# Forget sums and causal mask of a prompt's attention: from matrix products to copies by DMA and additions by VectorE

## The chip, the cores and the metric

One NeuronCore of a Trainium2 chip runs the whole kernel. The metric is the device time of one launch in microseconds (us).

## What is computed

One decoder layer for a prompt of 512 tokens and for 8 samples of one new token each, in float32. The input projection feeds three branches, the branches are gated and merged, and an output projection with a norm is added to the residual. The change touches only the prompt's attention. Its forgetting branch, with 8 heads of 64:

```
c = jnp.swapaxes(jnp.cumsum(logf, axis=1), 1, 2)                  # (B, 8 heads, 512)
s = einsum('bqhd,bshd->bhqs', qb, k) * scale + cb[..., :, None] - c[..., None, :]
p = _masked_softmax(s, kpos[None, :] <= qpos[:, None])
o = einsum('bhqs,bshd->bqhd', p, v)
```

The term of the query, `cb`, is the same along a row and falls out of the softmax, so the kernel adds only `-c`, one row of 512 values for each head. The sparse branch's selected-block and window attention use the same causal mask without such a term, and the memory branch uses neither.

## The kernel before

The program is a chain of stages, each a block with one instruction stream for each engine. A block ends when all its streams have ended. The ones that matter here are `project` (input projection), `middle`, `prompt` and `sample_and_merge`, in this order.

`middle` (551 us into the run it is over) does small work: the samples' compressed attention and its top-k, the first softmax of the samples' forgetting attention, the hidden layer of the prompt's compressed blocks, and the forget sums. Its SyncE (SP) queue loads weights `w1` into three parts of the tile `oT`: part i%3 holds step i of the four steps of `hidden`, so part 0 (rows 0 to 3 of `oT`) is used by steps 0 and 3, and part 2 (rows 8 to 11) by step 2. TensorE counts the steps in `hidden_done` (L896). VectorE writes the negated cumulative sums of all heads, `k.ncum`, [8 partitions, 512] (L1083). SP also copies a row `imp` (L851) and stores the log forget values (L853, L854) and waits for these stores at its end. The last instruction of the stage is VectorE's copy L1182.

`prompt` works in 56 units. A unit is a pair of heads (j = 0, 1) and a tile of 128 queries; with tile t the unit covers n = 128(t+1) keys, and a set is the four units t = 0 to 3 of one pair. Units 0 to 15 are the forgetting branch ("fox"), 16 to 47 the sparse branch (sets "slc" and "win" by turns), and 48 to 55 the memory branch, which has n = 256 and no mask. For each unit, by engine:

- TensorE, `scores(u)`: query times key (L1311); for fox the product of a one-hot column of the identity, spread over 128 columns, with `k.ncum`, accumulated into the same bank (L1315); then identity times `k.causal`, a 128 by 128 tile of zeros and large negative numbers, accumulated into the last 128 keys (L1319). Each of these is issued twice, once for each head; the trace shows two instructions for one such float32 product, so four in all.
- VectorE, `maximum(u)`: negated maximum over both heads' banks (L1398).
- ScalarE, `exponential(u)`: exponential with the row sum (L1445).
- VectorE, `normalise(u)`: reciprocal (L1402), gate for slc and win (L1405), scaling in place (L1409, twice).
- TensorE, `turn(u)`: transposes (L1330) into banks 4 and 5. VectorE copies those of head 0 to SBUF (`place`, L1416), ScalarE those of head 1 (L1453).
- TensorE, `values`: once a set, probabilities times values (L1350).

The order is written by hand. TensorE runs, for each u: scores(u+2), values of the set that has just ended, four page products (L1363), turn(u). VectorE runs maximum(u+2), normalise(u+1), place(u). ScalarE runs exponential(u+2), place(u). Scores(u+2) wait for the exponentials of u, since two pairs of score banks are used by turns; turn(u) waits for both copies of unit u-1.

The page products belong to the samples of the forgetting branch and ride along in units 4 to 48: 160 pages of 256 KB are loaded by SP (L1296) into eight places, freed pair by pair.

Of the kernel before, what the change touches and what calls it, by code (L numbers as in the profile page):

```python
# [25 lines left out]
ALU = mybir.AluOpType  # L26
# [10 lines left out]
H = 8  # L37
# [719 lines left out]
def middle(k):  # L757
# [4 lines left out]
    with ExitStack() as cx:  # L762
# [50 lines left out]
        grow_done = sem("a_grow_done")  # L813
# [22 lines left out]
        with nc.Block() as block:  # L836
            @block.sync
            def _(sp):
                def load_hidden(i):
                    for v in range(2):  # L840
                        for rows in halves:
                            sp.dma_start(w1[i % 3][rows, v, :, :], k.w_cmp1[0, v][:, i * STEP:(i + 1) * STEP, :]).then_inc(w1_in[i % 3], 16)

                sp.dma_start(bf[:, :], k.b_fgate.rearrange("a h -> h a")).then_inc(b_in, 16)
                sp.dma_start(gsel, k.selectors).then_inc(gsel_in, 16)
                for i in range(3):
                    load_hidden(i)
                sp.wait_ge(hidden_done, 1)
                load_hidden(3)
                sp.wait_ge(imp_out, 2)  # L850
                sp.dma_start(imp[:, :], flat.rearrange("o (n b) -> o n b", n=NG)).then_inc(imp_in, 16)  # L851
                sp.wait_ge(row_out, 2)
                sp.dma_start(rows_of(k.o_logf_p), lrow[:, :, :]).then_inc(out_done, 16)  # L853
                sp.dma_start(k.o_logf_s, k.slrow[:, :]).then_inc(out_done, 16)  # L854
                sp.wait_ge(out_done, 32)
# [344 lines left out]
def prompt(k):  # L1200
# [10 lines left out]
    U = len(units)  # L1211
    ends_group = lambda u: u.last and u.kind != "slc"
# [27 lines left out]
    with ExitStack() as cx:  # L1240
# [17 lines left out]
        pt_left, pt_right, o_done, out_done = (sem("f_" + n) for n in ("pt_left", "pt_right", "o_done", "out_done"))  # L1258
        o_out = [sem(f"f_o_out{i}") for i in range(2)]
        score = lambda u: [ps[2 * (u.no % 2)], ps[2 * (u.no % 2) + 1]]  # L1260
        both = lambda u: k.score_banks[:, 2 * (u.no % 2):2 * (u.no % 2) + 2, 0:u.n]
        pt_bank, o_bank, fv_bank = ps[4:6], ps[6], ps[7]
# [23 lines left out]
        with nc.Block() as block:  # L1286
# [18 lines left out]
            def _(te):  # L1305
                def scores(u):
                    if u.no >= 2:
                        te.wait_ge(e_done, 2 * (u.no - 1))
                    more = u.kind != "mem"
                    for j in range(2):  # L1310
                        last = nc.tensor.matmul(score(u)[j][:, 0:u.n], query(u, j), key(u, j), start=True, stop=not more,  # L1311
                                                skip_group_check=True)
                    if u.kind == "fox":
                        for j in range(2):
                            nc.tensor.matmul(score(u)[j][:, 0:u.n], k.ident[0:H, 2 * u.c + j:2 * u.c + j + 1].to_broadcast([H, P]),  # L1315
                                             k.ncum[:, 0:u.n], start=False, stop=False, skip_group_check=True)
                    if more:
                        for j in range(2):
                            last = nc.tensor.matmul(score(u)[j][:, u.t * P:u.n], k.ident, k.causal, start=False, stop=True,  # L1319
                                                    skip_group_check=True)  # L1320
                    last.then_inc(s_done, 1)
# [73 lines left out]
            def _(ve):  # L1395
                def maximum(u):
                    ve.wait_ge(s_done, u.no + 1)
                    nc.vector.tensor_reduce(nm[:, u.no, :], both(u), AX, ALU.max, negate=True).then_inc(m_done, 1)  # L1398
# [893 lines left out]
def hybrid_step(nc, x_prompt, x_sample, cache_nsa_cmp, cache_nsa_slc, state_nsa_win, cache_fox_kv, cache_fox_logf,  # L2292
# [59 lines left out]
    with ExitStack() as cx:  # L2352
# [20 lines left out]
        k.oT = sb("oT", [P, 12, T])  # L2373
        held, k.slrow = sb("srow", [NB, M_ALL]), sb("slrow", [NB, H])
# [60 lines left out]
```

## Time and profile before

| | |
|---|---|
| median of 3 runs | 1423.58 us (1414.3 to 1429.61) |
| the profiled execution | 1424.95 us |
| its span, first to last instruction | 1423.2 us |
| TensorE busy | 1204.9 us, 85% |
| VectorE busy | 802.0 us, 56% |
| ScalarE busy | 228.5 us, 16% |
| mean granted TensorE clock | 0.915 of full speed |

Busy times of the engines overlap. The profiled execution is one launch with the hardware profiler on; the last row says which share of its full 2.4 GHz TensorE was granted over the span.

### The profile page before, as it was taken

The page shows a single profiled execution, that of the slowest core. Times are in us where ns is not written, and L with a number is a line of the kernel's source. Part 1 is how long each engine was busy: PE and PEld are TensorE (multiplying, and loading weights), DVE is VectorE, ACT ScalarE, POOL GpSimd, SP SyncE. Part 2 cuts the span into 40 slices and gives each one's busy share as a digit, 9 for nine tenths or more (in the row PEclk, how much of TensorE's full clock was granted, in tenths as well). Part 3 has the DMA queues.
Part 4 walks back from the last instruction along what each step waited for, and adds up shares of the span by engine and source line. Part 5 has one row for each costly group of instructions (what it writes and reads, how often), then busy time and mean ns, then how long its engine had stood idle before and what let it go on. Part 6 is the DMA issues. An engine that isn't in the chain of part 4 may idle for free. (4 is left out here: it accounts for less than half of the span.)

```text
span 1423.2 us, 27444 instructions
## 1 busy us (share of the span) xinstructions
PE 1204.9 (85%) x10100; PEld 813.7 (57%) x10100; DVE 802.0 (56%) x1167; ACT 228.5 (16%) x692; POOL 173.1 (12%) x149
## 2 busy tenths in 40 slices
PE   0656677999999577999999888989899799999996
PEld 0655566887888455544444466766556364665542
DVE  1444331298989973335544547676776948544123
ACT  0010041112121111233333410110000000000023
POOL 0000000120000000000000073144051422410000
PEclk9978879999999775699999999999999989998998
DMA  8898524267888632187767194466578767657620
GB/s 221 248 314 240 169 85 148 89 222 217 277 280 295 213 78 75 49 306 226 258 233 233 60 291 152 149 193 229 160 231 260 248 209 234 221 176 270 244 93 31
DMA packets 205900, 282.01 MB, mean 198 GB/s; under 512 B 21749, under 2 KB 126734, under 8 KB 205254
## 3 DMA queue, kind: packets, MB, share of 16 engines
q1 hardware_dynamic: 109958, 202.40, 43.0%
q10 hardware_dynamic: 89376, 60.01, 14.8%
q0 software_dynamic: 6432, 17.83, 3.8%
q8 instruction: 80, 1.31, 0.4%
q14 instruction: 54, 0.44, 0.1%
HBM read 273.26 MB, written 11.11 MB: 200 GB/s over the span
## 5 line engine op out<-in xcount | busy, mean ns | idle before, releaser
L1735 PE MATMUL bank<-xnT,e_wg 128*128 128x260 f32 x1152 | 282.9, 405 | 0.0
L1735 PEld LDWEIGHTS bank<-xnT,e_wg 128*128 128x128 f32 x1152 | 230.8, 203 | 54.5 <-issue 15.8
L585 PE MATMUL score_banks<-xnT,oT 128*128 128x260 f32 (+1 forms) x864 | 196.8, 386 | 8.4 <-DMA oT<-in_w_in 8.4
L1719 POOL DMA_INDIRECT d_slc<-in_cache_nsa_slc,selrow x128 | 154.8, 1210 | 273.5 <-PE score_banks L1811 234.1
L585 PEld LDWEIGHTS score_banks<-xnT,oT 128*128 128x128 f32 (+1 forms) x864 | 161.3, 189 | 38.4 <-DMA oT<-in_w_in 8.7
L249 PE MATMUL score_banks<-c_cols,c_w 64*64 64x64 f32 (+1 forms) x4096 | 97.2, 256 | 96.6 <-issue 58.3
L249 PEld LDWEIGHTS score_banks<-c_cols,c_w 64*64 64x64 f32 x4096 | 92.4, 168 | 101.2 <-issue 101.2
L299 DVE COPY c_cols<-oT 128x1024 f32<-128x1024 f32 x48 | 49.6, 1159 | 92.5 <-DMA oT<-in_cache_nsa_cmp 67.1
L1398 DVE TENSOR_REDUCE f_pt<-score_banks 128x2 f32<-128x512 f32 (+3 forms) x56 | 45.1, 805 | 80.0 <-PE score_banks L1319 78.0
L1743 PE MATMUL bank<-oT,e_wb 128*128 128x512 f32 x192 | 89.0, 607 | 0.0
L1363 PE MATMUL bank<-mt,rpast 128*8 128x512 f32 x320 | 59.9, 601 | 6.1 <-DMA mt<-in_cache_fox_kv 5.0
L1416 DVE COPY f_pt<-bank 128x128 f32<-128x128 f32 (+2 forms) x68 | 27.6, 421 | 61.6 <-PE bank L1330 61.3
L1958 ACT ACTIVATE cst<-bank 128x260 f32<-128x260 f32 x36 | 14.0, 388 | 287.9 <-PE bank L1735 287.8
L1743 PEld LDWEIGHTS bank<-oT,e_wb 128*128 128x128 f32 x192 | 36.2, 194 | 41.9 <-issue 41.3
L2060 DVE TENSOR_REDUCE d_ss<-d_kpage 128x16 f32<-128x1024 f32 (+1 forms) x32 | 56.1, 1754 | 1.1
L2069 DVE TENSOR_TENSOR d_kpage<-d_kpage,d_qrow 128x2048 f32<-128x2048 f32 x24 | 54.7, 2281 | 2.8 <-DMA d_kpage<-in_cache_fox_kv 2.8
L2071 DVE TENSOR_REDUCE rpast<-d_kpage 128x32 f32<-128x2048 f32 x24 | 54.9, 2286 | 0.8
L1445 ACT ACTIVATE mnT<-score_banks,f_pt 128x256 f32<-128x256 f32 (+3 forms) x76 | 38.8, 515 | 79.5 <-DVE f_pt L1398 79.2
L745 DVE TENSOR_TENSOR oT<-oT,p_qrow 128x1024 f32<-128x1024 f32 x40 | 49.0, 1225 | 2.2 <-DMA oT<-in_cache_fox_kv 2.2
L745 DVE TENSOR_TENSOR mt<-mt,p_qrow 128x1024 f32<-128x1024 f32 x40 | 48.9, 1224 | 1.4 <-DMA mt<-in_cache_fox_kv 1.3
L747 DVE TENSOR_REDUCE sfe<-oT 128x16 f32<-128x1024 f32 x40 | 48.8, 1220 | 1.4
L747 DVE TENSOR_REDUCE sfe<-mt 128x16 f32<-128x1024 f32 x40 | 48.8, 1220 | 1.4
(390 smaller groups left out, 1447.1 us busy)
## 6 DMA issues: line engine op xcount, KB each, us to landing
mt<-in_cache_fox_kv SPq DMA_DIRECT2D x240, 256.0 KB, 3.8
d_kpage<-in_cache_fox_kv SPq DMA_DIRECT2D x96, 256.0 KB, 4.4
d_vpage<-in_cache_fox_kv SPq DMA_DIRECT2D x96, 256.0 KB, 3.6
oT<-in_cache_fox_kv SPq DMA_DIRECT2D x80, 256.0 KB, 3.8
e_wg<-in_w_in ACTq DMA_DIRECT2D x36, 512.0 KB, 5.1
oT<-in_cache_nsa_cmp SPq DMA_DIRECT2D x128, 128.0 KB, 3.8
oT<-in_w_in ACTq DMA_DIRECT2D x13, 1024.0 KB, 6.9
oT<-in_cache_nsa_cmp ACTq DMA_DIRECT2D x64, 128.0 KB, 3.7
```

What stands on the lines that cost most here:

```text
L249: return nc.tensor.matmul(hp[s][half][halves[v], 0:n], w1[rows, v, d, :], cols[s][rows, v, d, 0:n], start=d == 0, stop=d == HD - 1)
L299: nc.vector.tensor_copy(dst, src).then_inc(page_free[slot], 1)
L585: last = nc.tensor.matmul(pj[ch.n % 2][i][0:ch.w, 0:NM if ch.mem else TH], w[:, c, ch.off:ch.off + ch.w], rhs, start=c == 0, stop=c == DC - 1)
L745: nc.vector.tensor_tensor(slot, slot, qrow[b % 2][:, :].unsqueeze(1).to_broadcast([P, KR, BRW]), ALU.mult).then_inc(k_times, 1)
L747: nc.vector.tensor_reduce(k.sfe[:, b, g * KR:(g + 1) * KR, :], slot.rearrange("p n (h d) -> p n h d", h=H), AX, ALU.add).then_inc(k_free, 1)
L1363: last = nc.tensor.matmul(fv_bank[32 * i:32 * i + H, :], k.pfe[:, b, page, :], vpage[:, (n % VG) * KV + i % KV, :], start=g == 0, stop=g = ...
L1719: nc.gpsimd.indirect_dma_start(out=slc[:, b % 2, n, :], out_offset=None, in_=k.cache_slc, in_offset=bass.IndirectOffsetOnAxis(ap=k.selrow[ ...
L1735: last = nc.tensor.matmul(gate_bank[n % 2][:, 0:TH], wg[product % WR][:, c, :], k.xnT[:, c, part * TH:(part + 1) * TH], start=c == 0, stop ...
L1743: last = nc.tensor.matmul(z_bank[:, :], wb[n % 2][:, c, :], k.oT[:, (n % 3) * 4 + c, :], start=c == 0, stop=c == 3)
L2060: nc.vector.tensor_reduce(ss[:, first:first + tiles, g * R:(g + 1) * R].rearrange("p n r -> p r n"), product, AX, ALU.add).then_inc(small_ ...
L2069: nc.vector.tensor_tensor(pages, pages, qrow[:, 0, :].unsqueeze(1).to_broadcast([P, KR, BRW]), ALU.mult).then_inc(k_times, 1)
L2071: nc.vector.tensor_reduce(k.pfe[:, b - EARLY, g * KR:(g + 1) * KR, :], pages.rearrange("p n (h d) -> p n h d", h=H), AX, ALU.add).then_inc ...
```

## The change

The forget sums are spread to all partitions beforehand. In `middle`, once `k.ncum` is written (`cum_out`) and the weights in the place concerned are used up, SP issues eight DMAs. Each reads one head's row of `k.ncum`, 2 KB in one partition of SBUF, 128 times and writes it to the 128 partitions of one row of `oT` (heads 0 to 3 to rows 8 to 11 once step 2 of `hidden` is done, heads 4 to 7 to rows 0 to 3 once step 3 is). SP then waits for all eight, and only then issues the stores of the log forget values. In `prompt`, the products L1315 and L1319 are gone. VectorE's `maximum(u)` first adds the spread sums to both score banks in place (fox only, n values for each head), then the causal mask to the last 128 keys of both (all but memory units), each waiting for the one before by a semaphore, and then takes the maximum.

```diff
+                sp.wait_ge(cum_out, 1)
+                for h in range(H):
+                    if h % 4 == 0:
+                        sp.wait_ge(hidden_done, 3 + h // 4)
+                    sp.dma_start(k.bias(h), k.ncum[h:h + 1, :].unsqueeze(1).to_broadcast([1, P, T])).then_inc(bias_in, 16)
+                sp.wait_ge(bias_in, 16 * H)
                 sp.wait_ge(row_out, 2)
                 sp.dma_start(rows_of(k.o_logf_p), lrow[:, :, :]).then_inc(out_done, 16)
...
+    for u in units:
+        u.masks = sum(v.kind != "mem" for v in units[:u.no + 1])
...
+        own_block = lambda u: k.score_banks[:, 2 * (u.no % 2):2 * (u.no % 2) + 2, u.t * P:u.n]
...
-                    more = u.kind != "mem"
                     for j in range(2):
-                        last = nc.tensor.matmul(score(u)[j][:, 0:u.n], query(u, j), key(u, j), start=True, stop=not more,
-                                                skip_group_check=True)
-                    if u.kind == "fox":
-                        for j in range(2):
-                            nc.tensor.matmul(score(u)[j][:, 0:u.n], k.ident[0:H, 2 * u.c + j:2 * u.c + j + 1].to_broadcast([H, P]),
-                                             k.ncum[:, 0:u.n], start=False, stop=False, skip_group_check=True)
-                    if more:
-                        for j in range(2):
-                            last = nc.tensor.matmul(score(u)[j][:, u.t * P:u.n], k.ident, k.causal, start=False, stop=True,
-                                                    skip_group_check=True)
+                        last = nc.tensor.matmul(score(u)[j][:, 0:u.n], query(u, j), key(u, j), start=True, stop=True)
                     last.then_inc(s_done, 1)
...
                     ve.wait_ge(s_done, u.no + 1)
+                    if u.kind == "fox":
+                        forget = k.oT[:, (8 + 2 * u.c) % 12:(8 + 2 * u.c) % 12 + 2, 0:u.n]
+                        nc.vector.tensor_tensor(both(u), both(u), forget, ALU.add).then_inc(biased, 1)
+                    if u.kind != "mem":
+                        if u.kind == "fox":
+                            ve.wait_ge(biased, u.no + 1)
+                        nc.vector.tensor_tensor(own_block(u), own_block(u), k.causal.unsqueeze(1).to_broadcast([P, 2, P]), ALU.add).then_inc(masked, 1)
+                        ve.wait_ge(masked, u.masks)
                     nc.vector.tensor_reduce(nm[:, u.no, :], both(u), AX, ALU.max, negate=True).then_inc(m_done, 1)
...
+        k.bias = lambda h: k.oT[:, (8 + h) % 12, :]
```

## Rows read from the trace of the kernel before

**Rows 1.** Page, part 1: busy time, share of the span, instructions.
```profile
PE 1204.9 (85%) x10100; PEld 813.7 (57%) x10100; DVE 802.0 (56%) x1167; ACT 228.5 (16%) x692; POOL 173.1 (12%) x149
```

**Rows 2.** Prompt's attention: PE, PEld, DVE, ACT, POOL busy; clock, DMA share, GB/s.
```profile
553.00:815.00 262.00, 251.57 (x1319) 119.71 (x1319) 119.95 (x327) 90.53 (x310) 0.00 (x0) 0.91 0.59 195
```

**Rows 3.** Groups of instructions by line, 551 to 815 us: busy, mean ns, idle.
```profile
L1398 DVE TENSOR_REDUCE f_pt<-score_banks 128x2 f32<-128x512 f32 (+3 forms) x56 | 45.1, 805 | 80.0 <-PE score_banks L1319 78.0 <-PE score_banks L1311 1.8
...
L1319 PE MATMUL score_banks<-cst 128*128 128x128 f32 x192 | 38.1, 327 | 0.0
...
L1315 PE MATMUL score_banks<-ncum,cst 8*128 8x128 f32 (+3 forms) x64 | 28.9, 585 | 0.0
```

**Rows 4.** TensorE in order of time, full clock: start, duration (us).
```profile
601.21 0.49 PE L1311 MATMUL score_banks<-fm 64*128 64x128 f32 x4
...
616.85 1.98 PE L1315 MATMUL score_banks<-ncum,cst 8*128 8x512 f32 x4
...
618.75 0.71 PE L1319 MATMUL score_banks<-cst 128*128 128x128 f32 x4
...
619.40 1.04 PE L1363 MATMUL bank<-mt,rpast 128*8 128x512 f32 x8
...
620.96 0.49 PE L1311 MATMUL score_banks<-fm 64*128 64x128 f32 x4
```

**Rows 5.** Groups by shape, 600 to 780 us: busy us, mean ns.
```profile
L1398 DVE TENSOR_REDUCE f_pt<-score_banks 128x2 f32<-128x1024 f32 x10 | 12.3, 1225 | 19.1 <-PE score_banks L1319 19.1
...
L1398 DVE TENSOR_REDUCE f_pt<-score_banks 128x2 f32<-128x256 f32 x10 | 4.2, 424 | 2.6 <-PE score_banks L1319 2.6
```

**Rows 6.** VectorE by shape, whole span: one input in PSUM, and a PSUM write.
```profile
L1106 DVE TENSOR_TENSOR rpast<-rpast,bank 128x1280 f32<-128x1280 f32 x1 | 1.5, 1489 | 0.5 <-PE bank L964 0.5
...
L2178 DVE MEMSET bank<- 128x512 f32 x1 | 0.5, 485 | 1.3 <-PEq L2328 1.3
```

**Rows 7.** TensorE in order of time, 551 to 600 us, half clock.
```profile
551.36 0.80 PE L1311 MATMUL score_banks<-fm 64*128 64x128 f32 x4 [1.71 <-PEq L2328]
...
566.71 3.78 PE L1315 MATMUL score_banks<-ncum,cst 8*128 8x512 f32 x4
570.42 1.22 PE L1319 MATMUL score_banks<-cst 128*128 128x128 f32 x4
...
588.33 4.54 PE L1350 MATMUL bank<-f_pt,row 128*64 128x512 f32 x16
592.79 1.02 PE L1363 MATMUL bank<-mt,rpast 128*8 128x512 f32 x2
```

**Rows 8.** Middle stage in order of time.
```profile
511.13 0.46 SPq L853 DMA_DIRECT2D out<-a_lrow  x1
...
519.94 0.67 DVE L1083 TENSOR_SCALAR ncum<-score_banks 8x512 f32<-8x512 f32 x1
...
521.46 3.38 PE L896 MATMUL bank<-oT,cst 64*8 64x64 f32 x128
...
528.02 0.63 PE L896 MATMUL bank<-oT,cst 64*8 64x64 f32 x32
```

**Rows 9.** End of the middle stage in order of time.
```profile
549.68 0.68 DVE L1182 COPY cst<-bank 64x512 f32<-64x512 f32 x1 [1.16 <-PE bank L995]
```

**Rows 10.** Stretches: DMA share and GB/s, loads into 64 partitions.
```profile
499.00:499.50 0.50, 0.50 (x32) 0.50 (x24) 0.50 (x2) 0.06 (x1) 0.00 (x0) 0.50 1.01 229
```

**Rows 11.** Stretches: the same, pages into 128 partitions.
```profile
738.00:742.00 4.00, 4.00 (x24) 2.02 (x20) 1.75 (x4) 0.66 (x2) 0.00 (x0) 1.00 1.04 352
...
750.00:754.00 4.00, 2.13 (x8) 0.13 (x8) 1.56 (x6) 1.20 (x7) 0.00 (x0) 0.90 0.88 306
```

**Rows 12.** DMA issues, 488 to 560 us: KB each, us to landing.
```profile
oT<-in_w_cmp SPq DMA_DIRECT2D x16, 256.0 KB, 7.2
...
s_imp<-mnT SPq DMA_DIRECT2D x1, 4.0 KB, 2.1
```

**Rows 13.** Source line 1296, page loads.
```profile
DMA to landing us min/median/max: 2.5/3.9/8.5
```

More of the change, by code:

```diff
@@ L812, in middle @@
                                     "new_done", "pool_zero", "dup_done", "new_placed"))
-        grow_done = sem("a_grow_done")
+        grow_done, bias_in = sem("a_grow_done"), sem("a_bias_in")
         s_done, x, exp_done, imp_done, imp_out, t, first_turned, spread_done, rows_done, p_turned, pt_out, o_done, o_out, top = (
@@ L1258, in prompt @@
         pt_left, pt_right, o_done, out_done = (sem("f_" + n) for n in ("pt_left", "pt_right", "o_done", "out_done"))
+        biased, masked = sem("f_biased"), sem("f_masked")
         o_out = [sem(f"f_o_out{i}") for i in range(2)]
```

## The prediction

> **What bounds the kernel now.** I read the page's shares first, then the stretches, the groups by line, and at last the order of time, since a share over the whole span says nothing of one stage. TensorE leads with 85% [rows 1]. In the stretch of prompt's attention it is busy 251.6 of 262 us, VectorE 120, ScalarE 91, and the DMA engines 59% of the time [rows 2]. In the groups, VectorE's maximum has 80 us of idle time before it, 78 of them ended by the mask product L1319 [rows 3]: VectorE waits for TensorE, so products taken from TensorE's stream are worth something here. The mask products are busy 38.1 us and the forget products 28.9 us [rows 3].
>
> Two other things limit that. In the first 41 us of the stage, from 551.36 on, TensorE runs at 1.2 GHz: a forget product of 512 keys takes from 566.71 to 570.42, 3.7 us, against 1.9 at full clock (616.85 to 618.75) [rows 4, 7]. The clock rises to 2.4 GHz only while the first values products L1350 run, which begin at 588.33; the page products behind them at 592.79 have full speed [rows 7]. And the stage cannot begin before `middle` has ended, SP's queue included: today the last work is VectorE's copy, which ends at 550.36, and the first score product comes 1.0 us later [rows 7, 9].
>
> **Products removed and additions added.** At full clock a unit's mask products occupy TensorE from 618.75 to 619.40, 0.65 us, and the four forget products of a set 0.65 + 1.06 + 1.49 + 1.90 = 5.1 us (the ends by rows, the middle two in line with them) [rows 4]. A fox set thus loses 5.1 + 2.6 = 7.7 us of TensorE, an slc or win set 2.6.
>
> VectorE gets additions that the trace has not in this form: in and out in PSUM. [...] I take the price of the maximum at equal size, 0.42 us for 256 elements and 1.23 for 1024 [rows 5]. [...] A fox set gets 2 x (0.42 + 1.23) = 3.3 us for the sums and 4 x 0.42 = 1.7 for the masks, an slc or win set 1.7.
>
> Before, a set costs VectorE 3.3 us of maxima and (120 - 45.1) / 14 sets = 5.35 us of the rest [rows 2, 3], nearer 6 in a masked set, whose units have 320 keys in the mean and not 256. After, a fox set costs it 3.3 + 6 + 5 = 14.3 us, and 14.7 with the waits for each other's semaphores. TensorE's fox set takes 620.96 - 601.21 = 19.75 us today [rows 4], and 12.1 without the products. So in fox VectorE becomes the bound. The order by hand adds something: the copy of a set's last unit must be done before the values products, page products and transposes go on, and the next copy waits for those, during which VectorE runs dry for about 1 us. Followed through step by step, a set takes 15.7 us: 4.05 saved for each of the three later fox sets, 12.1 in all (with free additions 7.7 a set, with doubled ones nothing).
>
> In an slc or win set VectorE has 3.3 + 6 + 1.7 = 11 us against TensorE's 12.1 and more (the products of a fox set and the compressed part), so TensorE stays the bound, but at each set's end it waits some 1.2 us for VectorE's later copy, and the page loads have less time: the eight sets save 1.0 us each, 8 us (0 to 2.6 each).
>
> The first fox set lies at half clock. Seven forget and seven mask products go before the first L1350: twice 0.65 + 1.06 + 1.49, and once 1.90, 8.3 us at full clock and 15.7 at half (the row of 3.7 is a little under double); the masks, 1.15 each (570.42 and its 1.22 less the overlap), are 8.1 [rows 7]. TensorE's 37.0 us up to 588.33 would be 13.2. VectorE has by then the additions and maxima of units 0 to 5, 11.6 us, and the scalings of 0 to 4 and copies of 0 to 3, 6.5 by the 6 us a set: with 1.3 for the first score products ahead, 19.4 us. That is 17.6 us saved. Where the clock rises is taken as before, at these values products.
>
> **Gain of the stage:** 17.6 + 12.1 + 8 = 37.7, less 0.7 for page waits, 37 us; bounds 28 (dearer additions, no gain in slc and win) and 55 (cheap ones, TensorE bound nearly throughout). ScalarE, at 91 of 262 us, and the memory units are not touched.
>
> **The spread by DMA.** Eight DMAs write 8 x 128 x 2 KB = 2.10 MB. Their cover: steps 2 and 3 of `hidden` end at 521.46 + 3.38 = 524.8 and at 528.65, and the sums are there at 520.6 [rows 8]. SP can issue the first at 524.9. Behind the last SP has two stores, moved past the spread: 0.9 us of issue (twice 0.46) and about 2.1 to land, by the small copy s_imp [rows 8, 12]. So the spread costs nothing if it ends by 550.36 - 3.0 = 547.4. The fixed part of a DMA is the fastest page's 2.5 us [rows 13] less 256 KB at 352 GB/s [rows 11], 1.75 us: data flow from 526.65, and 20.7 us of cover mean 101 GB/s.
>
> Does a DMA whose source is one partition reach that? No row shows a large one. What the trace shows is that the rate follows the number of partitions on the SBUF side: loads of 256 KB into 64 partitions move 229 GB/s with all sixteen engines busy (share 1.01), pages of 256 KB into 128 partitions 352 (share 1.04) [rows 10 to 12]. [...] Below 22 there is the 4 KB of s_imp from one partition, 2.1 us less 1.75, some 12 GB/s, poor evidence as it is nearly all fixed time [rows 12]. I take the lane, and within it 27 GB/s, nearer to the 64-partition row because that one is narrow like this: 77.7 us, to 604.3; with the stores and the 1.0 us, the first score product at 608.3 in place of 551.36: 57 us later. With 28.6 it is 53, with 22 it is 75. Nothing hides this: TensorE, VectorE and ScalarE have ended `middle`, and SP's page loads stand behind it in the next block.
>
> [...]
>
> **Sum.** 1424.95 + 57 - 37 = 1445 us. The profiled run is 1.4 us over the median of 1423.58; I leave it there.
>
> **Rivals.** (A) The forecast: the reads of one partition go through one lane. Its own range: 1424.95 + 53 - 55 = 1423 to 1424.95 + 75 - 28 = 1472. 72%.
>
> (B) The other side: the spread is hidden. The reads run at 101 GB/s or more, for instance because sixteen engines draw on one partition as they do on 128; then 37 us are gained, 1388 us (1370 to 1397). For it: all sixteen engines get a share of each DMA, and the cover is long. Against it: the 64-partition rows, which have all engines busy too and yet lose a third of the rate [rows 10]. It decides from 101 GB/s on; the kernel breaks even at 57.7 us of data, 36 GB/s. 18%.
>
> (C) One partition gives less than a lane, as s_imp hints: 12 GB/s make 175 us, the stage starts 154 us late, 1542 us. 7%.
>
> (D) TensorE's clock. After a stretch with 2.13 of 4 us busy it fell to 1.2 GHz for some us (mean 0.90 in that stretch) [rows 11]. With VectorE as the bound TensorE pauses in each fox unit; if it stayed at 1.2 GHz there, the three later fox sets would need 2 x 12.1 = 24 us each and not 15.7, and 25 of the 37 us would be lost: 1470 us with A. 3%.
>
> **Chances and range.** Faster by over 1% (below 1409): B and a sliver, 0.19. Within 1%, about what a measurement can tell from no change: the part of A with a small shift and a large gain, 0.21. Slower: the rest of A, C and D, 0.60. The range 1384 to 1472 leaves out C, the lower half of B and the ends of A, near 2 in 10. A alone is 1423 to 1472.
>
> **What would show it.** Right: in `middle`, all engines idle from 550 to about 605, a DMA share near 1 with some 27 GB/s, the score products starting near 608; VectorE's additions at 0.42 to 1.23 us; L1311 of one fox set to the next 15.7 us apart; the first values products 19 us after the stage's first product, and the clock rising there. The DMA rate would make it wrong most easily: above 101 GB/s the stage starts at 551 as before. Next comes the half-clock part, if the clock rises before the values products or stays low past them, and the price of additions inside PSUM.

## The result

The change makes the kernel slower: a median of 1450.1 us (4 runs, 1447.76 to 1451.9) against 1426.59 (4 runs) for the kernel before on the same chip, ratio 1.0176 with a 95% interval of 1.0106 to 1.0247. The profiled run took 1449.06 us, its span 1447.3; before it was 1424.95 and 1423.2. All shifts below are differences of these two traces, in us:

| stretch | before | after | shift | forecast |
|---|---|---|---|---|
| start to first score product | 551.36 | 603.59 | +52.2 | +57 |
| to the first values product | 36.97 | 19.22 | −17.75 | −17.6 |
| next four intervals (three fox sets, the first slc set) | 80.7 | 71.6 | −9.1 | −13.1 |
| last seven intervals (slc and win), to the last values product | 127.0 | 125.1 | −1.9 | −7 |
| the rest of the program | 627.2 | 627.8 | +0.7 | +0.7 |
| sum | 1423.2 | 1447.3 | +24.1 | +20 |

An interval runs from one set's first values product to the next one's. There are twelve sets with masks and so eleven intervals behind the first values product: three of fox sets and eight of slc and win sets. The fourth ends with an slc set and has no forget products in it; its forecast of 1.0 is one of the eight in the 8 us. The last row but one carries the forecast's 0.7 for page waits.

The page of the changed kernel, part 1. TensorE's busy time fell by 52.2 us against [rows 1], VectorE's rose by 32.1, and the span rose all the same:

```profile
PE 1152.7 (80%) x9844; PEld 773.0 (53%) x9844; DVE 834.1 (58%) x1231; ACT 228.1 (16%) x692; POOL 173.7 (12%) x149
```

Where the time went is seen in SP's queue in order of time (start, duration), and in one stretch of the same trace (busy time of PE, PEld, DVE, ACT, POOL; granted clock, DMA share, GB/s):

```profile
523.45 56.30 SPq L856 DMA_DIRECT2D oT<-ncum  x8
600.52 0.43 SPq L859 DMA_DIRECT2D out<-a_lrow  x1
601.00 0.41 SPq L860 DMA_DIRECT2D out<-slrow  x1
```

```profile
550.00:600.00 50.00, 0.00 (x0) 0.00 (x0) 0.00 (x0) 0.00 (x0) 0.00 (x0) 0.50 0.84 28
```

The eight spread DMAs are issued from 523.45, and the stores behind them wait until 600.52. `middle`'s last copy is over at 549.02 (in [rows 9] it ends at 550.36, so what lies before was 1.3 us quicker here). For 50 us no engine computes, while the DMA engines are busy 84% of the time and move 28 GB/s. In [rows 11], at shares of 1.04 and 0.88, they move 352 and 306. The source line of the spread, with the duration of an issue (least, median and greatest, in ns) and the time to landing:

```profile
L856 SPq DMA_DIRECT2D oT<-ncum x8: 545/8971/9747, 523.4 to 570.0; - x8
...
DMA to landing us min/median/max: 12.0/31.0/32.4
```

The attention itself is shorter. Its beginning, TensorE in order of time, in the trace after:

```profile
603.59 1.65 PE L1320 MATMUL score_banks<-fm 64*128 64x128 f32 x8 [55.29 <-PEq L2336]
...
619.05 1.86 PE L1330 MATMUL bank<-cst,mnT 128*128 128x128 f32 x8
620.84 0.92 PE L1320 MATMUL score_banks<-fm 64*128 64x384 f32 x4
622.81 2.38 PE L1350 MATMUL bank<-f_pt,row 128*64 128x512 f32 x16 [1.05 <-ACT f_pt L1461]
```

And stretches of it (columns as above):

```profile
612.00:616.00 4.00, 1.05 (x8) 0.72 (x8) 3.90 (x8) 1.61 (x7) 0.00 (x0) 0.73 0.90 292
616.00:620.00 4.00, 3.55 (x15) 2.60 (x16) 3.20 (x9) 1.65 (x7) 0.00 (x0) 0.50 0.06 20
620.00:624.00 4.00, 2.95 (x15) 1.49 (x15) 3.86 (x10) 1.57 (x6) 0.00 (x0) 0.92 0.00 0
```

VectorE is busy 3.2 to 3.9 us of each four, so it sets the pace as forecast, and the first values product comes after 19.2 us; every trace with both additions, eight in all, has 19.2. The clock changed twice in the first part (means of 0.73 and 0.50) and rose with the score product at 620.84, just ahead of the values product, to stay up nearly all through the next four intervals (0.98 in the mean); that product takes 2.38 us and not the 4.54 of [rows 7].

VectorE's groups by shape show what the additions cost, one line for the forget sums (L1400), one for the masks (L1404), one for the maximum of the same width (L1406):

```profile
L1404 DVE TENSOR_TENSOR score_banks<-score_banks,cst 128x256 f32<-128x256 f32 x48 | 20.7, 431 | 14.7 <-PE score_banks L1320 14.1
L1406 DVE TENSOR_REDUCE f_pt<-score_banks 128x2 f32<-128x1024 f32 x12 | 14.7, 1224 | 0.4
...
L1400 DVE TENSOR_TENSOR score_banks<-score_banks,oT 128x1024 f32<-128x1024 f32 x4 | 4.9, 1230 | 2.1 <-PE score_banks L1320 2.1
...
L1400 DVE TENSOR_TENSOR score_banks<-score_banks,oT 128x256 f32<-128x256 f32 x4 | 1.7, 426 | 0.2 <-PE score_banks L1320 0.2
```

An addition with input and output in PSUM took as long as the maximum: 426 ns for 256 elements against the maximum's 425 in the same trace, 1230 for 1024 against 1224. The forecast took 0.42 and 1.23.

The 36.97 us of the kernel before are less firm. Two other traces have the same products in this part and nothing of VectorE's additions, and there the clock rose before the first values product. In before_half (described below), TensorE in order of time, the same kind of product at half clock and then at full clock:

```profile
560.25 2.07 PE L1316 MATMUL score_banks<-ncum,cst 8*128 8x256 f32 x4
...
582.58 1.12 PE L1316 MATMUL score_banks<-ncum,cst 8*128 8x256 f32 x4
...
588.12 2.37 PE L1351 MATMUL bank<-f_pt,row 128*64 128x512 f32 x16
```

That part took 32.05 us there, and 34.41 in spread_only, where the clock rose about 3 us ahead of the values product. Against the 19.2 the gain is thus 12.9 to 17.8 us, and what made the clock rise where it did stays open.

What the forecast had nearly left out is in the group of the page products, L1363 in both kernels: busy time, mean, and the idle time before them with what ended it. In the trace of before:

```profile
L1363 PE MATMUL bank<-mt,rpast 128*8 128x512 f32 x320 | 59.9, 601 | 6.1 <-DMA mt<-in_cache_fox_kv 5.0 <-issue 1.0
```

and after:

```profile
L1363 PE MATMUL bank<-mt,rpast 128*8 128x512 f32 x320 | 68.6, 625 | 20.5 <-DMA mt<-in_cache_fox_kv 18.3 <-issue 1.9
```

### The profile page after: what moved, and what is told of

It is laid out like the page before. It is cut to its first block and busy times, and to the rows that moved or that the text cites. A ratio compares the mean times of both kernels' runs of the same rounds, so it can differ in the third digit from the quotient of the medians.

```text
span 1447.3 us, 27006 instructions
## 1 busy us (share of the span) xinstructions
PE 1152.7 (80%) x9844; PEld 773.0 (53%) x9844; DVE 834.1 (58%) x1231; ACT 228.1 (16%) x692; POOL 173.7 (12%) x149
## 5 line engine op out<-in xcount | busy, mean ns | idle before, releaser
L1743 PEld LDWEIGHTS bank<-xnT,e_wg 128*128 128x128 f32 x1152 | 231.0, 203 | 54.7 <-issue 15.7
L1320 PE MATMUL score_banks<-fm 64*128 64x128 f32 (+3 forms) x192 | 41.9, 518 | 56.7 <-PEq L2336 55.3
L1363 PE MATMUL bank<-mt,rpast 128*8 128x512 f32 x320 | 68.6, 625 | 20.5 <-DMA mt<-in_cache_fox_kv 18.3
L1320 PEld LDWEIGHTS score_banks<-fm 64*128 64x128 f32 x192 | 15.6, 200 | 66.0 <-issue 62.8
```

The source lines that it names most:

```text
L1363: last = nc.tensor.matmul(fv_bank[32 * i:32 * i + H, :], k.pfe[:, b, page, :], vpage[:, (n % VG) * KV + i % KV, :], start=g == 0, stop=g = ...
L1743: last = nc.tensor.matmul(gate_bank[n % 2][:, 0:TH], wg[product % WR][:, c, :], k.xnT[:, c, part * TH:(part + 1) * TH], start=c == 0, stop ...
```

## The experiments

Three questions were open: what limits the spread, what each half of the change is worth, and where the 9 us went that fox, slc and win sets did not give. In the text, "fox" is the time from the first to the fifth set's values product (the first four intervals), "slc/win" from there to the last (the other seven). Each was read in one profiled execution; between kernels that do the same work these two differ by up to 3 us in fox (70.2 to 73.2) and 5 in slc/win (124.3 to 129.1), the time to the first values by up to 5 with the products (32.05 to 36.97), and smaller differences settle nothing.

### What limits the spread

**dram_spread.** The 16 KB of sums go to DRAM first, and each spread DMA reads its row there.

```diff
                 sp.wait_ge(cum_out, 1)
+                sp.dma_start(k.sums[:, :], k.ncum[:, :]).then_inc(bias_in, 16)
+                sp.wait_ge(bias_in, 16)
                 for h in range(H):
...
-                    sp.dma_start(k.bias(h), k.ncum[h:h + 1, :].unsqueeze(1).to_broadcast([1, P, T])).then_inc(bias_in, 16)
+                    sp.dma_start(k.bias(h), k.sums[h].partition_broadcast(P)).then_inc(bias_in, 16)
```

> The eight rows of sums go to a 16 KB scratch tensor in DRAM first, and each is spread from there; everything else is the changed kernel. Lane theory (one SBUF partition is read through one lane of 27 GB/s, and that is the whole loss): 2.1 MB move at 150 GB/s or more and are over before 547 us, the first score product comes near 550 and not at 603.6, and the time is 1450 less 54, about 1397 us, 0.98 of before. Rival, a spread of 2 KB rows to 128 partitions is slow wherever it reads: the stage starts late again by tens of us and the time stays above 1430.

Measured: 1393.33 us (1391.45 to 1397.77), ratio to the kernel before 0.9774, interval 0.9731 to 0.9816. SP's queue in order of time, and the stretches from the first spread issue on:

```profile
518.05 0.29 SPq L853 DMA_DIRECT2D sums<-ncum  x1
522.69 5.54 SPq L858 DMA_DIRECT2D oT<-sums  x8
533.84 0.40 SPq L861 DMA_DIRECT2D out<-a_lrow  x1
```

```profile
522.00:534.00 12.00, 6.18 (x212) 5.04 (x201) 8.31 (x30) 1.61 (x3) 0.00 (x0) 0.78 0.57 176
534.00:549.00 15.00, 8.91 (x72) 8.10 (x72) 7.77 (x27) 0.42 (x1) 0.00 (x0) 0.50 0.02 2
```

The same 2.10 MB to the same 128 partitions are there within 11.2 us of the first issue, 15 us before they are needed. The first score product comes at 549.17. So neither the broadcast nor the writes were the limit. What is left is the source: SBUF as such, or the one partition of it.

**two_hops.** Row h goes to 16 partitions spread over SBUF first, and seven copies of 16 source partitions each fill the rest.

```diff
-                    sp.dma_start(k.bias(h), k.ncum[h:h + 1, :].unsqueeze(1).to_broadcast([1, P, T])).then_inc(bias_in, 16)
+                        sp.dma_start(k.bias(h)[0:P:8], k.ncum[h:h + 1, :].unsqueeze(1).to_broadcast([1, 16, T])).then_inc(hop_in[i], 16)
...
+                    for r in range(1, 8):
+                        sp.dma_start(k.oT[r:P:8, four, :], k.oT[0:P:8, four, :]).then_inc(bias_in, 16)
```

> Each row is first copied to 16 partitions (0, 8, ..., 120), 0.26 MB out of the one partition, and then from those to the seven behind each, 1.8 MB out of sixteen partitions. Lane theory: first hop 9.7 us at 27 GB/s, second at 200 GB/s or more, some 9 us, all over by 547 us, time about 1397 us. Rival, copies within SBUF are slow whatever partitions they read: the second hop too runs near 27 GB/s, 67 us, and the time is 1440 us or more.

Measured: 1399.22 us, first score product at 555.03. SP's queue:

```profile
528.33 6.42 SPq L857 DMA_DIRECT2D oT<-ncum  x8
534.79 10.14 SPq L862 DMA_DIRECT2D oT<-oT  x14
547.42 0.44 SPq L865 DMA_DIRECT2D out<-a_lrow  x1
```

The source may stay in SBUF: with 16 source partitions instead of one, the bulk (1.84 MB) takes 12.6 us, from its first issue to the stores. So it was the single partition.

**same_lane and two_lanes.** Both send the same eight DMAs, four from SP and four from ScalarE's queue, after the same waits. In the first the two queues read rows 0 and 1, then 2 and 3, and so on, always two partitions of one group of four neighbours; in the second, one queue reads partitions 0 to 3 and the other 4 to 7. The waits, not shown below, put both queues at the end of `middle`.

```diff
-                for h in range(H):
+                for h in (0, 2, 4, 6):        # two_lanes: (0, 1, 2, 3)
...
+                for h in (1, 3, 5, 7):        # ScalarE; two_lanes: (4, 5, 6, 7)
+                    sc.dma_start(k.bias(h), k.ncum[h:h + 1, :].unsqueeze(1).to_broadcast([1, P, T])).then_inc(bias_in, 16)
```

> The spread as in the changed kernel, but started at the end of the middle stage (near 545 us) and issued from two queues at once: heads 0, 2, 4, 6 by SyncE, heads 1, 3, 5, 7 by ScalarE, so that at any time both queues read neighbouring partitions. Lane theory with four neighbouring partitions on one lane: 27 GB/s in all, 77 us, the stage starts near 545 + 77 + 5 = 627 us. Rival, the limit is one DMA or one queue at a time: two queues double it, 39 us, start near 589 us.

> As same_lane, but SyncE spreads heads 0 to 3 and ScalarE heads 4 to 7, so that the two queues read partitions 0 to 3 and 4 to 7 at the same time. Lane theory with four neighbours to a lane: two lanes, 54 GB/s, 39 us, start near 589 us. If eight neighbours share a lane, or if SBUF as a source is slow as a whole: 27 GB/s, start near 627 us as in same_lane.

Measured: 1478.35 and 1448.95 us. Stretches of same_lane, and of two_lanes while both queues were at work:

```profile
551.00:628.60 77.60, 1.06 (x4) 0.53 (x4) 2.48 (x7) 0.00 (x0) 0.00 (x0) 0.50 0.86 27
```

```profile
580.00:590.00 10.00, 0.00 (x0) 0.00 (x0) 0.00 (x0) 0.00 (x0) 0.00 (x0) 0.50 0.93 53
```

Two partitions out of rows 0 to 3, or out of rows 4 to 7, gave 27 GB/s together, as one did; a partition of each gave 53. The trace after has the same border. Its eight rows land some 10 us apart, row 3 at 564.0, and as row 4 follows the rate is 88 GB/s for one us; in no other us from 524 to 600 is it above 45:

```profile
563.00:564.00 1.00, 0.00 (x0) 0.00 (x0) 0.00 (x0) 0.00 (x0) 0.00 (x0) 0.50 1.05 88
```

At the same passage spread_only has 78 and same_lane 64. So the limit went with a group of four neighbouring partitions, some 27 GB/s for each of the two groups that were read.

The 53 did not last the whole transfer: two_lanes moved its 2.10 MB in 49.9 us (554.6 to 604.5), 42 GB/s in the mean, with 35 from 560 to 570 and 36 at the end. Its first score product came at 607.6 and not near the 589 expected, nearly 10 us of that by the later issue; same_lane's came at 631.7 for the 627 expected. Why the two queues did not overlap fully was not followed.

### What each half is worth

**spread_only.** The kernel before, with the change's spread added and nothing else; its result is not used.

```diff
+                sp.wait_ge(cum_out, 1)
+                for h in range(H):
...
+                sp.wait_ge(bias_in, 16 * H)
                 sp.wait_ge(row_out, 2)
```

> The kernel before, with the eight DMAs of the spread and their waits added and nothing else: the products stay, and nobody reads what is spread. Lane theory: the whole price of the spread is seen alone, the attention stage starts 54 us later than before and takes its 270 us, about 1479 us. Rival, part of the late start is the changed attention stage's own or is made good later: under 1465 us.

Measured: 1472.5 us, between the two expectations, first score product at 602.0, 34.4 us to the first values product, fox 82.2, slc/win 124.0. The spread alone costs 47.6 us over 1424.95, and the start of the stage moves by 50.6; of the difference 2.6 us are the earlier rise of the clock told above.

**masks_moved** has the masks as VectorE's additions and the forget sums still as products, with no spread; **forget_moved** the forget sums as additions (read from DRAM as in dram_spread), the masks still products.

In cuts, each against the changed kernel:

```diff
 # masks_moved
+                    if u.kind == "fox":
+                        for j in range(2):
+                            last = nc.tensor.matmul(score(u)[j][:, 0:u.n], k.ident[0:H, 2 * u.c + j:2 * u.c + j + 1].to_broadcast([H, P]),
+                                                    k.ncum[:, 0:u.n], start=False, stop=True, skip_group_check=True)
...
 # forget_moved
+                    if more:
+                        for j in range(2):
+                            last = nc.tensor.matmul(score(u)[j][:, u.t * P:u.n], k.ident, k.causal, start=False, stop=True,
+                                                    skip_group_check=True)
```

> Only the causal mask is moved to VectorE; the forget products stay with TensorE, and there is no spread. Theory of today (products count in full at half clock, little in fox sets, and not at all in slc and win sets, where the page loads set the pace): 8 us in the first set, 1 to 2 in each later fox set, nothing in the eight others, 11 to 14 us less than before, 0.990 to 0.992. Rival, TensorE's time counts everywhere: 38 us of mask products less, 0.973.

> Only the forget sums are moved to VectorE, spread through DRAM; the mask products stay. Theory of today: 15 to 16 us at half clock in the first set and some 2 in each later fox set, 20 to 22 us less than before, 0.985. If the two halves add up to the 31 us of dram_spread, each is worth what it takes out at half clock and the rest is shared. Rival, TensorE's time counts everywhere: 29 us less, 0.980.

Measured: masks_moved 1413.34 us (10 runs), ratio 0.9928 (0.9892 to 0.9964); forget_moved 1398.03, ratio 0.9824 (0.9756 to 0.9892). By stretch:

| | to first values | fox | slc/win |
|---|---|---|---|
| before | 36.97 | 80.7 | 127.0 |
| masks_moved | 29.1 | 74.6 | 122.9 |
| forget_moved | 20.6 | 72.1 | 123.9 |
| both (dram_spread) | 19.2 | 70.2 | 129.1 |

In the half-clock part the masks alone are worth 7.9 us and the forget sums 16.4; together they give 17.8, as VectorE is the bound by then. These three are differences to the 36.97 of one trace; to 32.05 they would be 4.9 us less each. masks_moved is just short of the 0.990 to 0.992 of its theory, and its interval leaves out the 0.973 of its rival; forget_moved's interval holds both its theory (0.985) and its rival (0.980). The two intervals of the whole programs that hold the forget sums overlap (0.9731 to 0.9816, 0.9756 to 0.9892): that the masks add something on top was not shown.

### Where the rest of the gain went

**half_pages, before_half and forget_half** are dram_spread, the kernel before and forget_moved with the same edit: each page load from the ninth on, when every place has been filled once, moves half its width (256 of 512 columns; the "128 of 256" in the expectation of before_half is a slip), and the other half keeps old values.

```diff
-                        sp.dma_start(vpage[:, (n % VG) * KV + i % KV, :].unsqueeze(1),
-                                     k.cache_fox[bass.ds(pg, 1), :, 1, :].rearrange("a p n -> p a n")).then_inc(v_in[n % VG], 16)
+                        w = BRW if n < VG else BRW // 2
+                        sp.dma_start(vpage[:, (n % VG) * KV + i % KV, 0:w].unsqueeze(1),
+                                     k.cache_fox[bass.ds(pg, 1), :, 1, 0:w].rearrange("a p n -> p a n")).then_inc(v_in[n % VG], 16)
```

> dram_spread, with each page load from the ninth on bringing only its first 256 of 512 columns (the other half of the samples' values is left out); every instruction of the engines stays. Theory that the page loads hold the pace of the later sets: a fox set goes from 17.5 to about 15.7 us, an slc or win set from 17.9 to 14 or 15, in all about 25 to 30 us, 1365 us. Rival, the order of work between VectorE and TensorE holds it: under 8 us, 1386 us or more.

> The kernel before, with every page load after the first ring of slots cut to half its width (128 of 256 columns; the other half keeps old values), everything else as it was. Same edit as the half-width page loads on the row-sums-from-DRAM kernel, where the sets from first values to last values fell from 199.3 to 179.1 us. Theory (in the kernel before, products with the masks and forget sums held the pace for most of each set, and pages only little): the sets fall from 207.7 to 198 to 204 us, so that the change's cut is worth 20 us once pages are out of the way. Rival (pages held the pace already and the removed products cost nothing): the sets fall to 180 to 188 us.

> The kernel that moved only the forget sums (read from DRAM), the masks staying products, with the page loads after the first ring of slots cut to half their width (the other half keeps old values). It differs from the half-width kernel measured before (fox sets 64.3 us, the eight sets of selected blocks and window 114.8) by the mask alone. Theory (with the pages out of the way a mask costs about as much as VectorE's addition as it did as a product; the kernel before with half-width pages had 112.7 in the eight sets): 111 to 117 us in the eight sets, and 64 to 68 in the fox sets. Rival (the removed mask products are worth 1 us a set, as the prediction had it): the eight sets take 121 us or more.

Measured: 1384.54, 1405.04 and 1380.26 us, one run each. The first lies between what its theory and its rival expected, the last agrees with its theory in both stretches.

| kernel | full pages: fox, slc/win | half pages: fox, slc/win |
|---|---|---|
| products for both (before) | 80.7, 127.0 | 78.6, 112.7 |
| masks as products (forget_moved) | 72.1, 123.9 | 65.7, 113.8 |
| no products (dram_spread) | 70.2, 129.1 | 64.3, 114.8 |

In half_pages the idle time that pages end falls from 20.0 us to 2.5 on TensorE and from 39.4 to 17.1 on its weight loads:

```profile
PEld bank L1366 <- DMA mt<-in_cache_fox_kv: 17.1, 25, 2.1
PE bank L1366 <- DMA mt<-in_cache_fox_kv: 2.5, 3, 1.7
```

Three things follow. The pages hold the pace in slc and win in every kernel, the one before included, by 10 to 14 us; before_half took 191.3 us from first to last values product where the theory had 198 to 204 of 207.7 and the rival 180 to 188, so both missed: pages and products each had a part. In fox, with the pages light, the change gives 14.3 us (78.6 to 64.3), with full pages 9.1 to 10.5. Not all of the difference is pages: the mean clock in fox is 0.96 in before_half and 1.00 in half_pages, some 6 us at half clock, which cost an estimated 3 us; and light pages shorten fox by 2.1 us in the kernel before and by 5.9 and 6.4 in dram_spread and forget_moved. So pages take something back, and how much one profile each doesn't settle. And in slc and win the removed mask products give nothing even with light pages (113.8 to 114.8).

That last point can be seen interval by interval, forget_half against half_pages, which differ by the mask alone. The seven intervals are 17.21, 16.46, 17.33, 16.69, 14.30, 17.46, 14.38 with the products and 19.13, 14.74, 20.74, 16.17, 13.29, 16.55, 14.20 without. Five get shorter, by 4.3 us in all, 0.87 each. The first and the third get longer by 5.3. The first, TensorE in order of time, with the mask products (forget_half):

```profile
639.09 0.49 PE L1324 MATMUL score_banks<-fm 64*128 64x128 f32 x4
639.51 0.71 PE L1328 MATMUL score_banks<-cst 128*128 128x128 f32 x4
641.24 1.02 PE L1372 MATMUL bank<-mt,rpast 128*8 128x512 f32 x2 [1.01 <-issue]
```

and without (half_pages):

```profile
638.77 0.49 PE L1323 MATMUL score_banks<-fm 64*128 64x128 f32 x4
641.20 1.53 PE L1366 MATMUL bank<-mt,rpast 128*8 128x512 f32 x2 [1.94 <-issue]
```

The page product starts at the same time in both, as it waits for something else (VectorE is busy 1.9 of the 2 us before it); the mask product had only filled the gap before it. Without it TensorE pauses 1.94 us instead of 1.01, and then the granted clock falls. Stretches of half_pages:

```profile
638.00:640.00 2.00, 1.26 (x12) 0.90 (x11) 1.93 (x5) 0.87 (x3) 0.00 (x0) 1.00 0.85 248
640.00:642.00 2.00, 0.80 (x2) 0.12 (x2) 1.90 (x8) 1.76 (x9) 0.00 (x0) 0.89 0.05 18
642.00:644.00 2.00, 2.00 (x3) 0.10 (x2) 0.46 (x2) 0.12 (x2) 0.00 (x0) 0.50 0.00 0
...
646.00:648.00 2.00, 2.00 (x11) 1.40 (x10) 0.56 (x1) 0.14 (x1) 0.00 (x0) 0.50 0.18 52
648.00:650.00 2.00, 2.00 (x15) 0.71 (x16) 1.17 (x3) 0.35 (x2) 0.00 (x0) 0.90 0.66 201
```

and the same place in forget_half, where the granted clock stays at 1.00:

```profile
640.00:642.00 2.00, 0.99 (x5) 0.15 (x3) 1.93 (x7) 1.92 (x9) 0.00 (x0) 1.00 0.00 0
642.00:644.00 2.00, 2.00 (x9) 0.20 (x8) 0.04 (x1) 0.00 (x0) 0.00 (x0) 1.00 0.00 0
```

The changed kernel itself does this in the same two sets, in the trace after:

```profile
700.00:702.00 2.00, 1.08 (x10) 0.72 (x9) 1.93 (x6) 1.04 (x3) 0.00 (x0) 1.00 0.81 279
702.00:704.00 2.00, 0.98 (x2) 0.12 (x2) 1.89 (x7) 1.71 (x9) 0.00 (x0) 0.65 0.36 136
704.00:706.00 2.00, 2.00 (x4) 0.10 (x2) 0.29 (x1) 0.00 (x0) 0.00 (x0) 0.50 0.00 0
...
738.00:740.00 2.00, 0.30 (x3) 0.30 (x3) 1.90 (x8) 2.00 (x9) 0.00 (x0) 1.00 0.73 222
740.00:742.00 2.00, 2.00 (x12) 2.00 (x12) 0.81 (x3) 0.43 (x3) 0.00 (x0) 0.54 0.89 306
```

Against before, its first and third slc/win intervals are 3.6 us longer together and the other five 5.5 us shorter.

One pair of traces could be chance, but all fourteen lean the same way. Their mean clock from the fifth to the last values product is:

| | mean granted clock, slc/win |
|---|---|
| with mask products | spread_only, before_half, forget_half 1.00; forget_moved 0.99; before 0.97 |
| masks as additions | stores_last 0.97; masks_moved 0.96; after, two_hops, same_lane, two_lanes, half_pages 0.93; dram_spread, copies_early 0.92 |

At 0.93 a stretch of 115 to 125 us has 16 to 18 us at half clock, which is worth at most 8 to 9 us: as much as the forecast had hoped to gain there. The falls are not always in the same intervals (two_hops and stores_last have no long one in the third), and one of 3 us also comes up with the mask products in place (before, forget_moved).

Of the 20.2 us that half_pages has gained at the end of the prompt's attention, the program keeps 10: its first sample-stage product comes 20.2 us earlier, its last 10.0. Between them samples' and weights' products come in another order; what they wait for was not followed. A gain in this stage is not all a gain of the program, though in the changed kernel the rest kept its length (+0.7).

**copies_early and stores_last** try to take other traffic away from the pages, both on dram_spread: the first issues the eight copies of the window state right after the spread, in the 15 us in which the DMA engines are idle, the second all output transfers after the last page load.

```diff
 # copies_early, in middle
+                for b in range(NB):
+                    sp.dma_start(k.o_win_s[b, 0:WIN - 1, :], k.state_win[b, 1:WIN, :]).then_inc(k.win_out, 16)
 # stores_last, in the attention
-                    if at // (2 * KV) % 2 == 1 and left:
-                        sp.dma_start(*left.pop(0)).then_inc(out_done, 16)
```

> The kernel with the row sums read from DRAM, and its eight copies of 511 KB from the window state to the output (4.1 MB) issued right after the spread instead of between the page loads. Theory (the page stream sets the pace of the prompt's attention): in the row-sums-from-DRAM kernel the DMA engines are 0.02 busy in the 15 us before the first score product, and 4.1 MB at about 250 GB/s is 16 us of queue that the pages no longer meet; the sets from first values to last values, 199.3 us there, shorten by 4 to 12 us, the program to 1381 to 1389 of 1393. Rival (pages wait for their own latency and for free slots, not for bytes): the sets stay within 2 us of 199, and the program within 3 us of 1393. Second rival: the first pages and the two logf stores queue behind the copies and the first values products start over 3 us later than 568.4, which gives the gain back.

> The kernel with the row sums read from DRAM, with all seventeen output transfers (9 stores, 8 copies) issued after the last page load instead of one for every fourth pair of loads. Theory (bytes beside the pages slow the page stream): the sets from first values to last values fall from 199.3 to 185 to 193 us; but 7.6 MB then run at the end, some 30 us at 250 GB/s, of which the last sets hide about 20, so the program ends at 1385 to 1400. Rival (latency and slots): the sets stay at 197 to 201 us and the program is 1393 or up to 15 later.

Measured: copies_early 1394.21 us, ratio 0.9799 (0.9757 to 0.9841), not told apart from dram_spread; the copies ran in the gap (257 GB/s from 534 to 549), but the sets took 198.2 us against 199.3, and the pages ended as much idle time of TensorE as before (19.3 us). The rival stands for these copies. stores_last 1400.18 us: its sets did shorten, to 188.4 us as its theory had it (though its clock, 0.97 in slc/win against dram_spread's 0.92, has a part in that), but its stage began 9.2 us later, behind a longer work ahead of it that the edit doesn't touch, and the program's end after the last memory unit is 7.2 us longer. The other output stores may cost the pages some us; one profile doesn't settle it, and as a version it wins nothing.

The best version remains dram_spread, 1393.3 us: 31 us under the kernel before and 57 under the changed one.

## Why the prediction was right, and where its terms were off

**The spread: right.** Predicted were 27 GB/s, an end at 604.3, and a stage 57 us late. From the data's assumed start at 525.2 to the stores at 600.52, 2.10 MB are 27.8 GB/s; the stage is 52.2 us late, 53.6 without the 1.3 that `middle` was quicker, and SP could issue at 523.45 and not 524.9. These shifts are no firmer than the start they are counted from: in the ten traces in which no spread holds the stage up, its first score product comes anywhere from 545.2 to 558.4. The 57 us stand on 27 GB/s for the reads of one partition and on 22 and 28.6 as their bounds. These were the author's estimates, and no row or run shows how they follow from the two widths, 229 GB/s into 64 partitions [rows 10] and 352 into 128 [rows 11]. What the runs showed in their place is 27.8 here, 27 out of one group of four in same_lane, and 53 out of two, rows 0 to 3 and rows 4 to 7, in two_lanes. That more partitions go with a higher rate held in all of them: 27 and 53, a mean of 146 out of sixteen partitions in two_hops (1.84 MB in 12.6 us), 229 and 352. Which other partitions go together was not tried. Rival B (hidden from 101 GB/s on) would have been the truth with another source: dram_spread reached it, at 1394.6 us in its profiled run for the 1388 predicted. The half-clock part and the sets gave 26.2 us there instead of 37, an earlier start and a shorter rest another 4.2. The gain of the sets is next.

**The half-clock part: right, and closer than it could know.** 17.6 predicted, 17.75 measured, by the mechanism given, VectorE's row of additions, maxima, scalings and copies: 19.4 us predicted for it, 19.2 measured in eight traces. The other side, the 37.0 of the products, was one trace's; with the 34.41 or 32.05 of the two others the gain is 15.2 or 12.9, so that agreement to 0.2 us is luck. In the changed kernel the clock rose 2 us before the first values product and not in it. Rival D did not come true in the fox sets: over the first four intervals the clock is 0.98 in the mean, with TensorE busy 62.4 of 71.6 us.

**The fox sets: mechanism right, 12.1 predicted, 9.0 measured.** The term stood on 15.7 us for each of three sets. With light pages the three take 17.1, 15.2 and 15.1 us, 15.8 in the mean. With full pages they take 18.2, 17.2 and 18.6. The step that fell short is "less 0.7 for page waits": TensorE's idle time ended by pages rose from 5.0 to 18.3 us in the stage. A faster consumer meets the same stream of loads; the DMA share in fox went from 0.71 to 0.80. The term is also counted too high: of the sixteen fox units seven have their forget products before the first values product, where the prediction takes them off already, and nine are left, 12.1 us by its own prices and not three times 5.1. The third set has the product of one unit alone. By the prediction's prices it loses 3.2 us less of TensorE's work and gets 2.1 less of VectorE's, and would save an estimated 2.9 us and not 4.05.

**The slc and win sets: 8 predicted, 2.1 measured.** That is over the eight intervals, and less than such a stretch varies by itself. The step that failed is "the eight sets save 1.0 us each". The size is right where the clock holds (0.87, in five of seven intervals with light pages). It leaves out that pages held this part already, by 14 us in the kernel before, and that in two sets the mask products filled a pause of TensorE: without them the pause is longer (1.94 us for 1.01 in the first, 2.05 for 0.93 in the third), and the granted clock falls to 0.50 for 7 to 10 us each time, which gives back 5.3 us (with light pages). Rival D had named this mechanism from [rows 11], but put it in the fox sets.

**The sum** missed by 4.1 us in the profiled run (1449.06 against 1445): the spread cost 4.8 less than predicted, and the stage gained 8.2 less (28.8 against 37), with 0.7 in the rest. Two errors of opposite sign partly cancelled, which is luck too.

## What to carry to other kernels

Before spreading a row over the partitions by DMA, count the partitions that it is read from: here the rate followed the source's groups of four neighbours, 27 GB/s from one group and 53 from two, and a detour of 16 KB through DRAM or a first hop to 16 partitions turned 77 us into 11 to 19. When products are taken from TensorE, ask what the loads will do when it asks for them sooner, and treat the removed product as a filler of a pause: a product that costs nothing where it stands may be what keeps the clock up (granted 1.00 with the mask products, 0.89 and then 0.50 without, at one place here). Take a stage's length before from more than one trace: the same products took 32 to 37 us here. When a gain is expected in a stage with several limits, lighten each limit alone in both kernels; a difference seen in one of them says little about which cause was whose.

## What the runs showed of the hardware beyond what was expected

- An issue held SP for as long as it took: the eight spread issues took from 545 to 9747 ns each and followed one another, 56.3 us in all, where the same eight from DRAM took 5.54. Had anything urgent stood behind them on SP, it would have waited for the issues, not only for the data.
- A DMA share of 0.84 to 0.93 said nothing of the rate: it stood beside 27 GB/s from one group of partitions (0.86), 53 from two (0.93), and 292 in the changed kernel's attention (0.90).
- A pause of 1.94 us behind a stretch with pauses (1.26 of 2 us busy) was followed by a fall of TensorE's granted clock from 1.00 to 0.50, for about 7 us, though it was busy nearly all of that time; behind one of 1.01 us at the same place, with TensorE busy 2.00 of the 2 us before, there was no such fall.
- The clock's rise is not tied to the program: with the same products TensorE ran at a granted clock of 0.50 for 37 us in the kernel before, and reached 1.00 some 26 us after the stage's first product in before_half.
- A float32 addition with input and output in PSUM took 426 ns for 256 elements and 1230 for 1024; a maximum over that width took 425 and 1224.
